# Neighbouring projections joined into one stage each, and a group norm moved beside a product

## The reference, cut to what matters

```python
hn = rms_norm(h, norm_mix_g[l])
proj = jnp.einsum('bsd,de->bse', hn, w_in[l])
za, zb, zc, xbc, dt_raw, g_raw = jnp.split(proj, SPLIT_POINTS, axis=-1)
ya = gmlp_mixer(za, ...)                   # gelu, norm, mixing over tokens
yb = rg_lru_mixer(zb, ...)                 # causal conv, gates, linear recurrence, times gelu(gate)
yc = ssd_mixer(zc, xbc, dt_raw, ...)       # causal conv, silu, scan by chunks, then:
    # y = y * silu(z); per group of 256 columns: y * rsqrt(mean(y * y) + EPS) * norm_g
merged = (gates[:, :, 0] * jnp.einsum('bse,ed->bsd', ya, w_branch_a[l])
          + gates[:, :, 1] * jnp.einsum('bse,ed->bsd', yb, w_branch_b[l])
          + gates[:, :, 2] * jnp.einsum('bse,ed->bsd', yc, w_branch_c[l]))
h = h + jnp.einsum('bsd,de->bse', merged, w_out[l])
hn = rms_norm(h, norm_mlp_g[l])
up = jax.nn.relu(jnp.einsum('bsd,df->bsf', hn, w_mlp_up[l]))
h = h + jnp.einsum('bsf,fd->bsd', up * up, w_mlp_down[l])
```

## Time and profile before

| | us |
|---|---|
| median of 3 runs | 3625.67 |
| lowest and highest | 3624.19, 3628.64 |
| span of the profiled execution (first to last instruction) | 3619.1 |
| TensorE matmuls busy | 3003.5 (83%) |
| VectorE busy | 1940.7 (54%) |
| ScalarE, GpSimd busy | 835.4 (23%), 883.0 (24%) |

### The profile page before, as it was taken

How to read it: one execution, slowest core, us unless ns; L and a number is a source line. 1 busy time by engine, 2 the same in 40 slices (tenths; PEclk the granted TensorE clock), 3 DMA queues, 4 the chain that set the end, 5 groups by cost and what they waited for, 6 DMA issues and landing times. The chain is left out here.

```text
span 3619.1 us, 28078 instructions
## 1 busy us (share of the span) xinstructions
PE 3003.5 (83%) x8564; PEld 1482.4 (41%) x8564; DVE 1940.7 (54%) x5001; ACT 835.4 (23%) x2159; POOL 883.0 (24%) x773
## 2 busy tenths in 40 slices
PE   6988988888888888777777887888777698988898
PEld 3434543333333333332343553334332456443663
DVE  1254567777777777677721646777776332332101
ACT  0222312222222222222223412222222130221100
POOL 0000014444444444444400004444444000000000
PEclk9997899999999999999988899999999899998999
DMA  5242339999999999999931539999999444333342
GB/s 203 71 178 83 101 121 427 427 427 427 426 420 418 418 426 419 426 420 424 411 125 53 193 133 422 427 427 427 426 427 427 162 134 129 123 116 111 123 150 111
DMA packets 242858, 1024.08 MB, mean 283 GB/s; under 512 B 46582, under 2 KB 51190, under 8 KB 142342
## 3 DMA queue, kind: packets, MB, share of 16 engines
q0 software_dynamic: 110592, 805.36, 53.0%
q1 hardware_dynamic: 131976, 216.47, 17.0%
q10 hardware_dynamic: 144, 0.52, 0.0%
HBM read 1021.15 MB, written 1.13 MB: 282 GB/s over the span
## 5 line engine op out<-in xcount | busy, mean ns | idle before, releaser
L1628 PE MATMUL l_peer_experts_acc<-l_peer_experts_ring,l_peer_experts_diag 128*128 128x512 f32 x1840 | 867.1, 614 | 209.7 <-ACT l_peer_experts_diag L1687 209.4
L1628 PE MATMUL l_peer_experts_acc<-weight_slots,l_peer_experts_diag 128*128 128x512 f32 x1232 | 588.5, 621 | 154.6 <-ACT l_peer_experts_diag L1687 154.5
L1848 DVE SCALAR_TENSOR_TENSOR l_peer_experts_ring<-l_peer_experts_ring,h_tiles 128x1024 f32<-128x1024 f32 x460 | 563.6, 1225 | 277.8 <-DMA l_peer_experts_ring<-in_expert_rows,l_peer_experts_picks 274.3
L1555 POOL DMA_INDIRECT l_peer_experts_ring<-in_expert_rows,l_peer_experts_picks x460 | 526.5, 1145 | 613.1 <-PE l_peer_experts_acc L1628 538.9
L1555 POOL DMA_INDIRECT weight_slots<-in_expert_rows,l_peer_experts_picks x308 | 355.3, 1154 | 1276.4 <-DVE l_peer_experts_picks L1777 841.2
L1628 PEld LDWEIGHTS l_peer_experts_acc<-l_peer_experts_ring,l_peer_experts_diag 128*128 128x128 f32 x1840 | 340.3, 193 | 705.3 <-issue 405.5
L1848 DVE SCALAR_TENSOR_TENSOR weight_slots<-weight_slots,h_tiles 128x1024 f32<-128x1024 f32 x308 | 377.3, 1225 | 186.5 <-DMA weight_slots<-in_expert_rows,l_peer_experts_picks 183.2
L1628 PEld LDWEIGHTS l_peer_experts_acc<-weight_slots,l_peer_experts_diag 128*128 128x128 f32 x1232 | 231.0, 196 | 488.4 <-issue 280.6
L1680 ACT ACTIVATE l_peer_experts_gel<-l_peer_experts_dots 128x2 f32<-128x2 f32 x384 | 78.4, 204 | 1187.8 <-DVE l_peer_experts_ring L1848 713.0
L1687 ACT ACTIVATE l_peer_experts_diag<-const_ident,l_peer_experts_wgt 128x128 f32<-128x128 f32 x768 | 266.5, 394 | 236.4 <-DVE l_peer_experts_wgt L1794 222.3
L1580 PE MATMUL l_peer_experts_queries<-h_t,l_query_weights 128*128 128x512 f32 (+3 forms) x512 | 172.3, 477 | 0.0
(11 more groups left out here) (464 smaller groups left out, 3349.9 us busy)
## 6 DMA issues: line engine op xcount, KB each, us to landing
weight_slots<-in_w_mod SPq DMA_DIRECT2D x24, 2048.0 KB, 7.7
weight_slots<-in_w_in SPq DMA_DIRECT2D x20, 2048.0 KB, 7.5
l_query_weights<-query_weights SPq DMA_DIRECT2D x16, 1024.0 KB
weight_slots<-in_w_mlp_up SPq DMA_DIRECT2D x8, 2048.0 KB, 7.6
weight_slots<-in_w_mlp_down SPq DMA_DIRECT2D x8, 2048.0 KB, 7.6
weight_slots<-in_gla_w_in SPq DMA_DIRECT2D x6, 2048.0 KB, 7.9
weight_slots<-in_ab_w_in SPq DMA_DIRECT2D x5, 2048.0 KB, 7.6
l_peer_experts_ring<-in_expert_rows,l_peer_experts_picks POOLq DMA_INDIRECT x460, 15.5
```

The lines of the kernel that those rows point to most:

```text
L1555: pool.indirect_dma_start(rows(b, k, None), None, uv, bass.IndirectOffsetOnAxis(ap=picks[:, b % 4, k:k + 1], axis=0)).then_inc(landing(b, ...
L1628: ins = nc.tensor.matmul(acc[:, b % 2, c * BANK:(c + 1) * BANK], diag[:, k % DIAGS, :], row[:, c * BANK:(c + 1) * BANK], start=(k == 0), s ...
L1848: nc.vector.scalar_tensor_tensor(row, row, 1.0, h[:, tile_of(b), :], ALU.mult, ALU.mult, accum_out=dots[:, b % 2, k:k + 1]).then_inc(dotte ...
```

## The change

`stage_linear` becomes a chain of one; `stage_chain` puts several projections (`Linear`) into one stage:

- ab_v and ab_qk are one stage, ab_vqk; c_q, c_k and c_v are c_qkv; b_xb, b_lg, b_za and b_wb are b_lru; b_xbc and b_z are b_xbcz; b_wa and b_wc are b_wac; b_mlp1 and b_mlp2 are b_mlp.
- One accumulator's halves alternate across all tiles of the chain (`turn`). TensorE waits in front of a tile for the count of copied-out tiles that frees its half.
- Where a later projection reads what work beside an earlier one makes, it waits on a counter (`ready`): b_wb for the recurrence (`recurred`), b_wc for the turned y, each block of b_mlp2 for two squared tiles. The convolutions, the gates' products and the last step of the recurrence wait for copied-out tiles in the same way.
- All side loads of a chain are issued at its start. Each engine does the side work of the projections in the chain's order.
- The stage b_norm goes; the group norm is the first part beside b_wa, and the turn stands two parts later. The gates' rows are loaded into a part of `b_sxc`, which is free by then.
- The loop over pairs of tiles is written out (b_mlp1 alone had one that runs more than once).

The norm has the same steps behind the same end of b_g, but in the stage of the products. The diff, cut to its core:

```diff
+    def place(self, weights, step0, turn0, shared0):
...
+        self.step0, self.turn0, self.shared0 = step0, turn0, shared0
+        self.both = self.func is None and len(self.groups(BANK)) > 1 and self.side is None and self.turned_out is None
...
+def stage_linear(nc, name, weights, *args, **kwargs):
+    stage_chain(nc, name, weights, [Linear(name, *args, **kwargs)])
+
+
+def stage_chain(nc, name, weights, links):
...
     with stage(nc, name) as st:
...
+        acc = st.ps("acc", [P, min(2, turns), max(ln.n_banks for ln in links), BANK])
...
-            pe.wait_ge(weights.loaded[slot], weights.count(i if isinstance(i, int) else half, turn))
-            if b == 0:
-
-                pe.wait_ge(act_out, t + 1)
-                if both:
-                    pe.wait_ge(dve_out, t + 1)
...
+            pe.wait_ge(ln.weights.loaded[slot], ln.weights.count(i, i // 2))
+            if b == 0 and turn >= 2:
+
+                pe.wait_ge(act_out, turn - 1)
+                if ln.shared0 + t >= 2 and (ln.both or t < 2 and ln.shared0):
+
+                    pe.wait_ge(dve_out, ln.shared0 + t - 1)
+            if ln.ready:
+                ln.ready(pe, t, b)
...
-        pairs = full // 2 if kb == 1 and full >= 4 and not side else 0
...
+                for ln in links:
+                    for part in ln.parts:
+                        if "sync" in part:
+                            part["sync"](sp)
+                for ln in links:
+                    for i in range(ln.steps):
+
+                        sp.wait_ge(mm_done, ln.step0 + i + 1)
+                        ln.weights.load(sp, i + 2)
...
             @block.vector
             def _(dve):
...
+                for ln in links:
+                    for t in range(len(ln.widths)):
+                        if ln.both:
+                            empty(dve, ln, dve_out, t, True)
+                        if ln.square is not None:
+                            done = ln.out[:, 4 * t:4 * t + 4, :]
+
+                            dve.wait_ge(act_out, ln.turn0 + t + 1)
+                            nc.vector.tensor_tensor(done, done, done, ALU.mult).then_inc(ln.square, 1)
+                    for at in range(len(ln.parts)):
+                        do(ln, "vector", dve, at)
...
-            link(nc.vector.tensor_tensor(some(gate, g), some(gate, g), some(den, g), ALU.mult))
+            if g == 0:
+                gate_ready(dve)
+            nc.vector.tensor_tensor(some(gate, g), some(gate, g), some(den, g), ALU.mult).then_inc(recurred, 1)
...
+            stage_chain(nc, "ab_vqk", weights, [Linear("ab_v", h_t, tiles, v_aug, by_head=P), Linear("ab_qk", h_t, tiles, qk_t, feature=True)])
...
+                    def conv(st):
+                        def emptied(dve):
+
+                            dve.wait_ge(st.act_out, 2)
+                            dve.wait_ge(st.dve_out, 2)
...
+                                                       a["lru_lambda_2"][0], lambda pe: pe.wait_ge(st.convolved, 4), lambda dve: dve.wait_ge(st.act_out, 4))
...
+                    stage_chain(nc, "b_lru", weights, [
+                        Linear("b_xb", h_t, tiles, xr, feature=True),
+                        Linear("b_lg", h_t, tiles, gate, feature=True, func=ACT.Gelu_apprx_tanh, side=conv),
+                        Linear("b_za", h_t, tiles, uv, func=ACT.Gelu_apprx_tanh, side=lru),
+                        Linear("b_wb", gate, tiles, branches[1], ready=lambda pe, t, b: pe.wait_ge(at[0].recurred, 2))])
...
+                            Linear("b_z", h_t, tiles, zs, func=ACT.Silu,
+                                   side=lambda st: conv_parts(nc, st, "sconv", xr, 2 * KC, a["ssd_conv_w_2"][0], a["ssd_conv_b_2"][0], xc, True, conv,
+                                                              ready=lambda dve: dve.wait_ge(st.act_out, 4))[0])])
...
-                    stage_head_norm(nc, "b_norm", y, range(LT), S_GROUPS, D // S_GROUPS, a["ssd_norm_g_2"][0], None, None, y, EPS2)
...
+                    def norm_and_turn(st):
+                        norm, normed = head_norm_parts(st, y, range(LT), S_GROUPS, D // S_GROUPS, a["ssd_norm_g_2"][0], y, EPS2)
+                        turns, st.turn_emptied, n_turns = turn_parts(nc, st, ident, y, y_t, range(LT), KC, ready=lambda pe: pe.wait_ge(normed, LT))
+                        at[0] = st, n_turns
+                        return [norm, {}] + turns
+
+                    stage_chain(nc, "b_wac", weights, [
+                        Linear("b_wa", ya_t, tiles, branches[0], side=norm_and_turn),
+                        Linear("b_wc", y_t, tiles, branches[2], ready=lambda pe, t, b: pe.wait_ge(at[0][0].turn_emptied, at[0][1]),
+                               side=lambda st: gate_parts(nc, st, g, a["b_gate_2"][0], branches, hn, lambda dve: dve.wait_ge(st.act_out, 2),
+                                                              xc[:, 0:12, :].rearrange("p (i k) t -> p i (k t)", i=3)))])
...
+            stage_chain(nc, "b_mlp", weights, [
+                Linear("b_mlp1", h_t, tiles, up, feature=True, func=ACT.Relu, square=squared),
+                Linear("b_mlp2", up, tiles, down, ready=lambda pe, t, b: pe.wait_ge(squared, 2 * b + 2))])
```

269 lines of the change are left out of this document (117 added, 152 removed).

## The result

| | before | after |
|---|---|---|
| median, us | 3625.67 (3 runs), 3627.06 with one more beside after | 3578.95 (4 runs) |
| lowest and highest | 3624.19, 3628.64 | 3578.55, 3579.23, and the fourth run 4010.26 |
| profiled execution: span | 3619.1 | 3577.4 |
| profiled execution: own time | not given | 3579.23 |

The account below looks back on a forecast made before the run. In the last block TensorE's products and the pauses between them bound it; the DMA-busy expert gathers lay out of reach. Gains at the joints less 3.0 us of clears summed to 33.2: 3625.7 - 33.2 = 3592.5 us, range 3583 to 3603.

Parts of the forecast that it names:

- The wait for the recurrence: In front of b_wb TensorE still waits 4.3 us, now on a counter; gain 2.7 us, bounds 1.9 to 4.8.
- the Silu that takes the end of b_z: At b_z's end ScalarE's Silu, not the product, comes last, at 3120.7 against 3123.64; gain 2.9 us instead of 5.
- the start of b_wa 5.3 us after b_g: b_wa starts 5.3 us after b_g's last matmul; 8.7 us idle saved, 1.3 more clock lost, gain 7.4.
- The norm's cover: The norm runs beside b_wa, ending at worst 18.6 us in, before the turn at 22 us, so stays covered.
- rival 2: Side loads in b_lru hold up b_lg's weights, 13.8 us late: gain 19.4, 3606.2 us, chance 0.05.
- Rivals 4 and 5: Each tile waits for the previous tile's copy-out, 3644.5 us, chance 0.03; barriers weren't the cost, pauses refill, 3621 us, chance 0.04.
- Rival 1: The low clock comes at other pauses, left or moved, giving back 6.5 us: 3599.0 us, chance 0.15.
- 6.6 us above the span. I carry the difference over: The timed median, 3625.67 us, lay 6.6 us above the profiled span of 3619.1; that difference was kept after the change.
- put down to the sequencer after the barrier: Idle of 1.87 to 13.97 us before each product's first matmul was read as the stage barrier's cost.
- The six pauses of the earlier trace: Low clock behind pauses at c_q, b_za, b_wb, b_wa, b_wc and b_mlp2, 1.44 to 2.94 us lost at each.
- The clears: GpSimd clears 37 more semaphores at the ends of b_lru, b_xbcz and b_wac; cost 3.0 us.
- rival 3: More gain: b_wb's clock stays up (+2.1), b_wa starts as it did (+1.3), clears free (+3.0): 3586.1 us, chance 0.13.

Follow-up runs that it names:

- experiments 2 and 3: All joints undone and norm its own stage, in the changed code: 3616.96 us; changed kernel with unused counters raised at each product stage's start: 3582.25 us.
- experiments 5 and 8: Changed kernel with b_mlp1 and b_mlp2 apart: 3582.7 us; changed kernel with extra VectorE products in the norm ahead of b_xb: 3579.14, 3579.71 and 3576.86 us.

## Why the prediction was wrong in size

**What held.** By the steps of the sum, against the first trace of the kernel before: ab_qk 2.5 for 2.4; the three products of the first block 6.3 for 6.1; b_wa and b_wc net of clears 1.5 for 1.4; the MLP 5.3 for 5.3, and 4.6 + 0.6 when undone. The wait for the recurrence, the Silu that takes the end of b_z, the start of b_wa 5.3 us after b_g, the turn's copies: each came where it was said and within 0.15 us. The norm's cover held: its row load kept VectorE for 2.62 us, and the norm still ended some 13 us ahead of the turn:

```profile
3235.64 0.18 DVE L1394 RECIPROCAL b_wac_head_rs<-b_wac_head_rs 128x4 f32<-128x4 f32 x1 [2.62 <-DMA b_wac_head_rows<-in_ssd_norm_g]
...
3253.03 1.04 PE L415 MATMUL b_wac_turn<-const_ident,b_uv 128*128 128x128 f32 x8
```

The side loads of b_lru did not hold up b_lg's weights, so rival 2 fell. Each of the three small column loads kept SyncE 1.5 to 1.6 us at its issue and landed 3.4 to 5.6 us later; the last was issued 8 us after b_xb's first matmul, inside the slack. The Trainium skill (DMA: Bandwidth & Descriptors, Rules for kernel authors) says that a load with a strided last dimension becomes one descriptor for each element; these rows agree in kind, since the loads are of a few KB. b_mlp1 takes 110.75 us without its loop and took 110.77 with it, so what the Trainium skill says of taken branches, that they break the sequential prefetch (Runtime: NRT & Kernel Launch, Instruction fetch mechanics), made no difference that this trace shows. Rivals 4 and 5 fell with the idle times: none in front of the tiles of a chain, and the joined pauses gone. (The stages have 37 tiles by the kernel's own list, not 39, so rival 4's price was 50 us, not 52.) Rival 1 fell in sum: of its 6.5 us only 2.1 came back, in b_g.

**The step from the span to the median failed (4.8 us).** "6.6 us above the span. I carry the difference over" took two different things for one offset. 1.8 us are fixed; the other 4.8 were the luck of that one execution. Executions of the kernel before spread from 3613 to 3631 us over all batches, and a single span is one draw from that. The sum priced the pauses and the clock of that one execution and took the gain off the median, as if the 4.8 us between them would stay in the changed kernel. They did not: the changed kernel's first three executions lie at 3578.55 to 3579.23 us, the profiled one among them, and its later four have a median of 3577.36. The second trace of the kernel before, 2.7 us longer, has 3.0 us more of low clock from b_xb on, so a large part of such a difference is low clock; the rest of the 4.8 is not traced to a place. The bounds had 4.5 us for the runs' spread, but the sum was not centred on it.

**The start of a stage was missing from what a stage costs (2.0 to 2.9 us).** The sum took a stage's price from the joined places only. The start counters also left the stages that were not joined. Six of the 11 show it, 2.0 us in all (ab_v, ab_o, c_q, c_g and b_xb 0.30 or 0.31 each, as 2.04 to 1.73 for b_xb; b_mlp1 2.23 to 1.74); three more have it inside pauses that other terms lengthened or shortened; in front of b_out and ab_qkv nothing was gained. That these 2 to 3 us are the counters' rests on experiments 2 and 3, the half of it by argument. The diff shows the lines removed, and the earlier trace rows name them as releasers; the step "put down to the sequencer after the barrier" read past both.

**The clock, place by place, was mis-sized both ways (2.6 us net).** Behind the pauses that are left the forecast was near: b_wb 2.1 lost for 1.7 measured, b_wa 2.8 for 2.6, b_wc none for none. The step "the Silu is last next" stopped there: with it b_g's pause grows from 2.69 to 4.95 us, and the clock behind it falls. The stretches after, behind the pauses of b_wb, b_g, b_wa and b_out in turn:

```profile
2968.72:2974.70 5.98, 5.98 (x10) 2.61 (x11) 0.00 (x0) 0.00 (x0) 0.00 (x0) 0.71 0.51 199
3101.12:3107.90 6.78, 6.78 (x11) 2.96 (x12) 0.27 (x1) 0.00 (x0) 0.00 (x0) 0.69 0.44 132
3229.76:3235.60 5.84, 5.84 (x8) 2.52 (x9) 3.18 (x18) 1.66 (x3) 0.00 (x0) 0.55 0.84 250
...
3301.73:3305.70 3.97, 3.97 (x10) 1.82 (x11) 0.00 (x0) 0.00 (x0) 0.00 (x0) 1.00 0.01 2
```

0.31 x 6.78 = 2.1 us were lost in b_g, which the forecast had not. Against it stand 2.3 us won in b_out, 1.1 in b_xbc and 0.8 in b_xb, in places whose low clock of before I had not looked at, since no edit stood there. The six pauses of the earlier trace rows were a selection. Time lost to TensorE's low clock, the granted clock laid over its busy time from b_xb on, was 23.4 us before and 15.0 after. The sum had 4.3 of those 8.4, and 1.4 more, b_z's, could not arrive, since the Silu ends that stage. The second trace of the kernel before lost 26.4 us: against it the net would be 5.6, so the size of this term is that of one trace.

**Smaller ones.** The clears were taken a little high: 3.0 us, where 0.93 + 0.56 + 0.15 were measured at b_xbc, b_merge and the linear attention, and some more inside b_g's 4.95. A wait for a small load beside b_xbc shrank by 0.6 us (4.99 to 4.42). What then is left of the 8.5 us, about 2, lies in the expert stages (1711.38 to 1711.00, and 902.03 to 899.95 us from the linear attention to b_xb, with c_g's start in it) and is within what they do by themselves. It stays open.

**The range** ended at 3583. Its upper half guarded against a clock given back, and below the forecast it had only rival 3's three terms and 4.5 us for the runs' spread. The errors that came, offset, starts and clock, all pushed down, and the offset alone used up that spread.

## What to carry to other kernels

When a pause is put down to another engine's sequencer, open the line it names: here it was the raising of a counter at the stage's start, beside the barrier; with it went some 0.3 us in most stages. Price a joint as idle time plus the low clock behind it, then ask for the next pause it lengthens and the clock behind that one. Where a barrier goes and a dependence stays, move what paces the dependence: one group of matmuls earlier was worth 6.5 us here. And price pauses and low clock from more than one profile: the one execution read here was 5 us faster than the median, and what it lacked went with the change as well.

## What the runs showed of the hardware

The low clock follows TensorE's pauses, but not their lengths alone. Behind the same 3.09 us of idle b_g's first group took 10.11 us in one kernel and 7.10 in another; behind the same 1.46 us b_out took 27.70 us in one and 30.40 in another. Two traces of the changed kernel have the same pattern to 0.2 us, and from b_g on it stays when all is shifted by 1.2 or 2.5 us; but ahead of b_g it changed by 2.0 us with the shift, and by as much in a trace without one (experiments 5 and 8). Such a shift cost nothing that the medians show (3579.71 and 3576.86 us against 3578.95 and 3577.36). A counter more to clear costs 0.06 to 0.07 us at its stage's end (0.11 at b_xbcz's), raising counters at the start 0.15 to 0.2 us.
